# A rebuilt front of a hybrid mixer kernel: half of the first modulation on TensorE, low weight halves on VectorE, the residual's scale and bias rows on GpSimd in one block

## What is computed

```python
x = layer_norm(x, ln0_g, ln0_b)
mod = silu(c) @ ada_w + ada_b
sh1, sc1, g1, sh2, sc2, g2 = split(mod, 6)
h = x * (1.0 + sc1) + sh1
z = h @ w_in
y = concat([pool_mixer(z[:, :512]), rglru_mixer(z[:, 512:1024], z[:, 1024:])]) @ w_out
x = layer_norm(ALPHA * x + g1 * y, ln1_g, ln1_b)
h = x * (1.0 + sc2) + sh2
y = peer(h, wq, k1, k2, u, v)
x = layer_norm(ALPHA * x + g2 * y, ln2_g, ln2_b)
```

## Time and profile before

| | us |
|---|---|
| median of three runs | 1901.21 (1898.95 to 1901.32) |
| the profiled execution, device time | 1901.77 |
| its span in the trace | 1900.0 |
| TensorE busy in the span | 1766.3 |
| VectorE busy in the span | 1218.4 |
| ScalarE busy in the span | 633.8 |
| GpSimd busy in the span | 604.3 |

### The profile page before, as it was taken

One profiled execution on the slowest core, in us unless ns is written; L12 is line 12 of the kernel. 1 busy time (PEld: TensorE's weight loads), 2 busy tenths in 40 slices (PEclk: granted clock), 3 DMA queues, 4 the chain that ended last, 5 costly groups with the idle time before them and its releaser, 6 DMA issues.

```text
span 1900.0 us, 24874 instructions
## 1 busy us (share of the span) xinstructions
PE 1766.3 (93%) x8396; PEld 1433.9 (75%) x8396; DVE 1218.4 (64%) x2200; ACT 633.8 (33%) x809; POOL 604.3 (32%) x266
## 2 busy tenths in 40 slices
PE   2779889998989998999999999999999999999994
PEld 2565468887867777878888888888888888888883
DVE  7995879999979980035555555555555555555567
ACT  1215133323269982232222222222222222222221
POOL 1541245383410013452222333333322223333333
PEclk9889989999989999999999999999999999999997
DMA  9433330043339997453444343344444444333311
GB/s 384 188 142 156 114 122 1 28 148 129 126 107 285 280 283 267 150 199 150 150 149 148 142 138 137 141 139 149 149 149 149 149 149 146 135 132 147 144 38 45
DMA packets 136109, 288.89 MB, mean 152 GB/s; under 512 B 8160, under 2 KB 73824, under 8 KB 133376
## 3 DMA queue, kind: packets, MB, share of 16 engines
q1 hardware_dynamic: 134352, 283.15, 42.4%
q0 software_dynamic: 1424, 4.85, 0.7%
q10 hardware_dynamic: 288, 0.29, 0.0%
HBM read 235.83 MB, written 52.43 MB: 152 GB/s over the span
## 4 chain that ended last, share of the span: by engine, by line
PE 53%; DVE 2%; ACT 0%; issue 0%; DVEq 0%; ACTq 0%
PE bank L778 18%; PE bank L780 18%; PE bank L779 18%; DVE acc L1410 0%; DVE xt L1438 0%; DVE w_full L1351 0%; DVE st L1439 0%; DVE nmean L1427 0%; DVE w_full L1434 0%; DVE xt L1413 0%; ACT xt L745 0%; DVE xt L1447 0%; DVE acc L1367 0%; DVE xt L1448 0%; DVE u_lo L1308 0%
## 5 line engine op out<-in xcount | busy, mean ns | idle before, releaser
L489 POOL TENSOR_TENSOR v_lo<-v_raw,v_hi 128x1024 fp32r<-128x1024 f32 x128 | 307.7, 2426 | 719.9 <-ACT v_hi L691 719.9
L778 PE MATMUL bank<-h_hi,u_hi 128*128 128x512 f32 x1248 | 499.1, 400 | 15.7 <-POOL u_lo L484 11.3
L780 PE MATMUL bank<-h_hi,u_lo 128*128 128x512 f32 x1248 | 492.1, 394 | 0.0
L779 PE MATMUL bank<-h_lo,u_hi 128*128 128x512 f32 x1248 | 492.0, 394 | 0.0
L1367 DVE TENSOR_TENSOR acc<-acc,bank 128x512 f32<-128x512 f32 x496 | 329.2, 685 | 148.6 <-PE bank L780 148.5
L778 PE MATMUL bank<-v_hi,w_hi 128*128 128x512 f32 x1024 | 400.3, 391 | 8.9 <-DVE w_lo L1361 7.9
L779 PE MATMUL bank<-v_lo,w_hi 128*128 128x512 f32 x1024 | 399.8, 390 | 0.0
L780 PE MATMUL bank<-v_hi,w_lo 128*128 128x512 f32 x1024 | 399.8, 390 | 0.0
L691 ACT ACTIVATE v_hi<-v_raw 128x1024 fp32r<-128x1024 f32 x128 | 128.5, 1052 | 545.5 <-PE bank L780 545.5
L1351 DVE TENSOR_TENSOR w_full<-gelu_out,gate_in 128x512 f32<-128x512 f32 x64 | 45.2, 706 | 384.9 <-ACT gelu_out L707 214.4
L778 PEld LDWEIGHTS bank<-h_hi,u_hi 128*128 128x128 f32 x1248 | 238.5, 191 | 67.6 <-POOL u_lo L484 11.6
(11 more groups left out here) (171 smaller groups left out, 1691.9 us busy)
## 6 DMA issues: line engine op xcount, KB each, us to landing
u_raw<-ut_dram SPq DMA_DIRECT2D x128, 512.0 KB, 3.3
v_raw<-v_dram SPq DMA_DIRECT2D x128, 512.0 KB, 5.8
gate_in<-gates_dram SPq DMA_DIRECT2D x64, 512.0 KB, 6.9
wbuf<-ada_w_dram SPq DMA_DIRECT2D x12, 2048.0 KB, 14.5
early_dram<-gelu_out SPq DMA_DIRECT2D x64, 256.0 KB, 2.2
gates_dram<-wbuf SPq DMA_DIRECT2D x4, 4096.0 KB, 16.0
gates_dram<-arena SPq DMA_DIRECT2D x4, 4096.0 KB, 16.0
early_in<-early_dram SPq DMA_DIRECT2D x64, 256.0 KB, 6.2
```

What stands on the lines that cost most here:

```text
L489: pool.tensor_tensor(v_lo[:, s, :], v_raw[:, s, :], v_hi[:, s, :].bitcast(F32), ALU.subtract).then_inc(s_vlo, 1)
L778: pe.matmul(out, a_hi, b_hi, start=(k == 0), stop=False)
L779: pe.matmul(out, a_hi, b_lo, start=False, stop=False)
L780: return pe.matmul(out, a_lo, b_hi, start=False, stop=(k == n - 1))
```

## The change

The front is written anew on every engine; the queries, the ranking, the scatter and the main loop stand as they were.

- Ada pieces 0 to 3: VectorE weighs chunks 0 to 3 only. TensorE takes chunks 4 to 7 as products of one column straight from the piece (`upper_modulation`, 16 products a piece). The two sums are added.
- The low halves of the 12 z weight tiles are made by VectorE (`low_weights_of`), and a third buffer exists for tile 2. ScalarE makes the full h of every other chunk. z 0 and z 1 are computed together, chunk by chunk; four banks instead of two hold z.
- GpSimd has during z only the 8 `affine` instructions, as one block, from the end of the first transposes on.
- Gates of the recurrence, ada 4 and 5 and the rest are interleaved with z; ada 4 to 9 all go through slot 3. Gelu is applied where z 8 to 11 leave their banks. The product of gate i and the convolved x goes from GpSimd to VectorE.
- Ada 6 to 9 are spread over the mixer output. The second h is made in two parts: three token blocks, then the last.
- Ada 10 and 11, the second gate, go to the stage of 20 expert tiles, with their DMAs behind the second tile of that stage. The zeroing of `acc` goes there too, from GpSimd to VectorE.

```diff
-PIECES = ([("ada", j) for j in range(4)] + [("win", 1), ("ada", 4), ("ada", 5), ("win", 0), ("ada", 6), ("ada", 7)]
-          + [("win", 2), ("ada", 8), ("ada", 9), ("wout", 0), ("wout", 1), ("ada", 10)]
-          + [("wq", 0), ("ada", 11), ("wq", 1), ("wq", 2), ("wq", 3)])
+PIECES, SLOT_OF = zip(
+    (("ada", 0), 0), (("ada", 1), 1), (("ada", 2), 2), (("ada", 3), 3),
+    (("win", 1), 0), (("win", 0), 1), (("win", 2), 2), (("ada", 4), 3), (("ada", 5), 3),
+    (("wout", 0), 1), (("ada", 6), 3), (("wout", 1), 2), (("ada", 7), 3), (("wq", 0), 0),
+    (("ada", 8), 3), (("ada", 9), 3), (("wq", 1), 3), (("wq", 2), 1), (("wq", 3), 2))
+NSPLIT = 4
+HALF_K = KD // 2
+MOD_UPPER = 64
...
 SLOTS = 4
-SLOT_OF = [n % SLOTS for n in range(len(PIECES) - 5)] + [0, 3, 1, 2, 3]
 CAND_A = 4 * K
 CAND = CAND_A + (K - 4) * 4
...
             for n, (name, j) in enumerate(PIECES):
                 slot = SLOT_OF[n]
-                if (name, j) in (("win", 0), ("wq", 3)):
-                    sp.wait_ge(s_hlo, KD if name == "win" else 2 * KD)
-                if slot in SLOT_OF[:n]:
+                if (name, j) == ("wq", 0):
+                    sp.wait_ge(s_lru, 1)
+                elif slot in SLOT_OF[:n]:
                     sp.wait_ge(*used_up(max(m for m in range(n) if SLOT_OF[m] == slot)))
                 sp.dma_start(piece_buf[:, slot], src[name][j]).then_inc(s_piece[slot], 16)
...
+                if s == 1:
+                    sp.wait_ge(s_scmm, 4 + S // 4)
+                    for g in range(2):
+                        sp.dma_start(late_ada[g], ada_w[10 + g]).then_inc(s_late[g], 16)
...
             def affine(nth, n):
                 if n == 0:
-                    pool.wait_ge(s_tr, KD * (nth + 1))
+                    pool.wait_ge(s_tr, 3 * KD if nth else KD)
                     pool.wait_ge(s_rows, 32 * (nth + 1))
...
             def lo_weights(n):
                 pool.wait_ge(s_wthi, n + 1)
                 pool.tensor_tensor(u_lo[:, n % 2], weights(n), u_hi[:, n % 2].bitcast(F32), ALU.subtract
                                    ).then_inc(s_wtlo, 1)
-            lo_weights(0)
-            lo_weights(1)
+            pool.wait_ge(s_piece[0], 32)
+            load_rows("ln0_g", "ln0_b")
+            load_gate_bias("gate1_b")
             for n in range(2 * TB):
                 affine(0, n)
-                lo_weights(n + 2)
-            for n in range(2 * TB + 2, NZ):
-                lo_weights(n)
             pool.wait_ge(s_x0, TB)
             load_rows("ln1_g", "ln1_b")
...
             centre(0)
+            centre(1)
+            pool.wait_ge(s_wtlo, NZ)
+            lo_weights(NZ)
+            lo_weights(NZ + 1)
             pool.wait_ge(s_ymm, 2 * TB)
             pool.wait_ge(s_yres, 2 * TB)
             load_gate_bias("gate2_b")
...
+            def upper_modulation(j):
+                wait_piece(pe, "ada", j)
+                for m in range(4):
+                    for k in range(HALF_K, KD):
+                        pe.matmul(bank[7][:, 4 * j + m:4 * j + m + 1], piece("ada", j)[:, k, m * P:(m + 1) * P],
+                                  silu_c[:, k:k + 1], start=(k == HALF_K), stop=(k == KD - 1))
...
-            transposes(0, BANKS_X, range(4))
-            for j in range(4):
-                modulation(j)
-            transposes(0, BANKS_X, range(4, KD))
-            for n in range(12):
-                pe.wait_ge(s_wtlo, n + 1)
-                if n >= 2:
-                    pe.wait_ge(s_zev, n - 1)
-                for k in range(KD):
-                    if n == 0:
...
+            transposes(0, BANKS_X, range(len(BANKS_X)))
+            pe.wait_ge(s_silu, 1)
+            upper_modulation(0)
+            modulation(0)
+            upper_modulation(1)
+            modulation(1)
+            upper_modulation(2)
+            modulation(2)
+            upper_modulation(3)
+            modulation(3)
...
+            pe.wait_ge(s_wtlo, 2)
+            for k in range(KD):
+                if k + len(BANKS_X) < KD:
+                    transposes(0, BANKS_X, range(k + len(BANKS_X), k + len(BANKS_X) + 1))
+                pe.wait_ge(s_hlo, k + 1)
+                z_chunk(0, k)
+                z_chunk(1, k)
...
+            z_tiles(2, 6)
...
+            mixer_output(0, range(NG))
+            mixer_output(1, range(NG))
+            mixer_output(0, range(NG, KD))
+            mixer_output(1, range(NG, KD))
+            modulation(6)
+            modulation(7)
+            mixer_output(2, range(KD))
+            mixer_output(3, range(KD))
+            modulation(8)
+            mixer_output(4, range(KD))
+            mixer_output(5, range(KD))
+            modulation(9)
+            mixer_output(6, range(KD))
             transposes(1, BANKS_H)
-            pe.wait_ge(s_yres, 2 * TB)
-            modulation(10)
-            modulation(11)
+            mixer_output(7, range(KD))
+            pe.wait_ge(s_sc, 2)
+            transposes(2, BANKS_L)
...
                 expert_inputs(0, c, BANKS_SCATTER[c % GT], c - (GT - 1))
+                if c == T_RANK + T_SCATTER + AT_GATE2:
+                    pe.wait_ge(s_scev, 4 + S // 4)
+                    modulation(10)
+                    modulation(11)
...
+            def partial_modulation(j, chunks=range(KD)):
...
+                end = HALF_K if j < NSPLIT else KD
+                for k in chunks:
...
+            def low_weights_of(n):
+                hi, lo = split_of(n)
+                ve.wait_ge(s_wthi, n + 1)
+                ve.tensor_tensor(lo, weights(n), hi.bitcast(F32), ALU.subtract).then_inc(s_wtlo, 1)
...
             for j in range(4):
-                partial_modulation(j)
+                partial_modulation(j, range(HALF_K))
+            low_weights_of(0)
             read_mod(0, 16, 4)
+            link(ve.tensor_tensor(mod[:, 0:16], mod[:, 0:16], bank[7][:, MOD_UPPER:MOD_UPPER + 16], ALU.add))
             scales(0, 8, "ln0_g", "ln0_b", scale1, bias1)
-            low_input(0, BANKS_X, scale1, bias1)
-            partial_modulation(4)
-            partial_modulation(5)
+            low_input(0, BANKS_X, scale1, bias1, range(0, 1))
+            low_weights_of(1)
+            low_input(0, BANKS_X, scale1, bias1, range(1, KD))
+            low_weights_of(2)
             ve.wait_ge(s_expl, 1)
...
-            add_gate_row(0)
-            partial_modulation(6)
-            partial_modulation(7)
+            low_weights_of(3)
+            low_weights_of(4)
+            ve.wait_ge(s_wtlo, 4)
+            convolve((0, 1))
+            low_weights_of(5)
+            convolve((2, 3))
+            low_weights_of(6)
+            partial_modulation(4, range(HALF_K))
+            low_weights_of(7)
+            partial_modulation(4, range(HALF_K, KD))
+            partial_modulation(5)
...
+            add_gate_row(0)
             for g in range(NG):
                 ve.tensor_tensor(bufs[g + 1][:, g, PAD_P:2 * PAD_P], ramp[:, g, :], zp[:, g, PAD_P:2 * PAD_P],
                                  ALU.subtract).then_inc(s_pooly, 1)
...
+                ve.wait_ge(s_zev, NZ - 4 + c + 1)
+                ve.tensor_tensor(y_lru[:, c, :], gr[:, c, :], zg[:, c, :], ALU.mult).then_inc(s_lru, 1)
+            partial_modulation(6)
+            partial_modulation(7)
...
+            ve.wait_ge(s_rowg, 2)
+            residual(0)
+            partial_modulation(8)
+            residual(1)
+            partial_modulation(9)
+            link(head_means(0))
+            scaled_means(0)
+            residual(2)
+            read_mod(24, 40, 10)
+            scales(24, 32, "ln1_g", "ln1_b", scale2, bias2)
+            low_input(1, BANKS_H, scale2, bias2)
+            link(head_means(1))
+            scaled_means(1)
+            residual(3)
+            low_input(2, BANKS_L, scale2, bias2)
...
+            link = Chain(ve, s_cg).link
+            partial_modulation(10)
+            ve.wait_ge(s_part, GATE_PIECES[2] + 1)
+            ve.memset(acc[:, :, :], 0.0).then_inc(s_zacc, 1)
+            partial_modulation(11)
+            add_gate_row(1)
```

More of the change, by code:

```diff
@@ L845, in queries @@
                     for k in range(KD):
-                        if first:
-                            pe.wait_ge(s_hlo, KD + k + 1)
+                        if first and half == 0:
+                            pe.wait_ge(s_hlo, 2 * KD + k + 1)
                         mm = thrice(bank[half][:, :], k, KD, ((u_hi[:, half, k, :], u_lo[:, half, k, :]),
@@ L1114, in _, with convolve @@
-            add_gate_row(0)
-            partial_modulation(6)
-            partial_modulation(7)
+            def convolve(channels):
+                for t in range(CONV_W):
+                    for c in channels:
+                        w = vec("conv_w", 4 * t + c)
+                        shifted = zx[:, c, PAD_C - CONV_W + 1 + t:PAD_C - CONV_W + 1 + t + S]
+                        if t == 0:
+                            ve.wait_ge(s_zev, c + 1)
```

(30 more changed lines are left out.)

365 lines of the change are left out of this document (189 added, 176 removed).

## The result

The changed kernel takes 1904.99 us, median of 9 runs (1903.05 to 1906.53), beside 1900.69 for the kernel before on the same chip (9 runs, 1898.78 to 1902.12). The ratio is 1.0024, with a 95% interval of 1.0014 to 1.0033: slower by 4.6 us. The forecast was 1900 us, with chances of 0.44 for faster by over 0.2%, 0.34 for the same and 0.22 for slower. The profiled execution has a span of 1903.5 us, 3.5 more than before.

A forecast was written before the change was run, and what follows sets the result against it. The front was taken to wait for VectorE, with a microsecond won at the first query a microsecond of the whole. 1901.8 - 4.1 (front) + 1.7 (gate sums) + 1 (load) = 1900.4, taken as 1900; range 1884 to 1908.

The forecast's parts named there:

- Scale rows: Front's start: with TensorE's one-column records at the lower clock level, rows ready at 55 us, 9 later than before.
- The 36 and the 18: Scale rows: us that all 160 one-column records take at the lower and at the upper clock level.
- the 3 us of credit: Scale rows: 3 us taken off for one-column records directly behind the transposes, still at the upper clock level.
- The block on GpSimd: Front, during z: eight instructions of 2.4 us, taking turns with VectorE one for one, from 65 until about 87.
- TensorE's wait before z 3: Front: TensorE idles 11.6 us after z 2 ends at 78.7, then starts z 3 slowly.
- the wait for ada 7: Mixer output: ada 7 ready 7.6 us after issue at 168; a TensorE wait at L805 of 7 or more shows it.
- First query: Front's end: first query starts at 246.6 against 250.75 before, 4.1 us earlier.
- the distance to the first ranking: From first query to first ranking: should stay 28 us.
- The clock rival: Front: clock stays up through one-column products, scale rows 14 us earlier than walked, total 1887; chance 0.25.
- The stage of 20 tiles: Gate sums +1.7 us, 4 MB load +1 us; ada 10 and 11 and the zeroing hidden under VectorE's idle 87.8.
- The store rival: Stage of 20 tiles: the new load holds up gelu stores, ScalarE waits 10 to 14 us, total 1912; chance 0.13.
- GpSimd's block costs nothing: Front: VectorE gets its small instructions in between, z 3 would not wait, 11 us earlier there, total 1891; chance 0.09.

The follow-up runs named there:

- h3: The changed kernel unaltered, measured once more on the same chip as another run: 1906.38 us, ratio 1.0038 to the kernel before.
- g1: On top of e3: VectorE weighs ada 0 to 3 whole, TensorE does no one-column products of upper halves: 1887.00 us, ratio 0.9934.
- g3: On top of e3: the 17 small decay instructions of VectorE moved ahead of the scale rows: 1888.94 us, ratio 0.9945.
- h1: On top of e3: two unread products of 512 columns behind each of the 16 groups of one-column products: 1908.88 us.
- g2: On top of e3: one unread product of 256 columns behind each of the 16 groups of one-column products: 1908.95 us, ratio 1.0041.
- e3: Changed kernel with the 4 MB loaded in four 1 MB parts behind tiles 5, 7, 9, 11, gate sums behind tile 16: 1896.80 us, ratio 0.9983.
- e4: Changed kernel with e3's spread load and the zeroing of acc in 8 pieces, one behind each chunk of ada 11: 1900.02 us, ratio 0.9992.

## Why the prediction was wrong

Its time, 1900, was 5 us short, and with it the sign. By its own steps:

- *Scale rows*: 55 predicted, 55.95 seen. That it is so close has some luck in it: the 160 one-column records took 34.1 us at the lower level where 36 were reckoned, and the 3 us of credit did not come in this execution. The 36 and the 18 are about 160 times the record of the earlier trace rows and of the earlier trace rows, 0.23 and 0.115 us. That the level falls through one-column products was the author's assumption there; rows 4 alone do not show it. In its place stands h3: the first 32 records took 3.72 us, the next 32 of the same line 6.97. The block on GpSimd 65 to 87, seen 65.7 to 86.2; TensorE's wait before z 3 11.6, seen 10.0; the wait for ada 7 7.6, seen 7.8 on VectorE and 3.8 of it on TensorE at L805, where 7 or more was to show it, so this mark failed while the piece was 1.3 us early. First query 4.1 us earlier, seen 4.5; the distance to the first ranking fell from 28.3 to 27.3 us. The front was right in mechanism and nearly in size, and g1 and g3 each took away the cause that it named and got the time back.
- *The clock rival* (1887) did not occur: the one-column records of the first modulation took 0.21 to 0.23 us. h1 and g2 show that what TensorE did there decided the level (0.12 us a record against 0.21). Only the 3 us of credit behind the transposes come and go: in this trace the first 32 records take 6.83 us, in h3's 3.72, with the same code. TensorE's busy time does not tell the two levels apart: in h3 TensorE was busy for 8.00 of 8 us from 30 to 38, and the granted clock was 0.50; in h1 it was busy for 32.00 of 32 us, at 0.12 us a record.
- *The stage of 20 tiles* is the step that failed. The sum had +1.7 for the gate sums (seen 1.77) and +1 "between none and 14" for the 4 MB. The 4 MB and the zeroing together cost 8.2 in one stall. Two things were missing. The slack was counted in buffers (four tiles of `u`, two gelu buffers), not in time: the low half of `u` has 1.4 us to spare per tile, and the store was 3.7 us late. And the zeroing and ada 11 were put under VectorE's 87.8 idle us at no cost: they cost VectorE nothing, but with ada 11 ready behind the zeroing, a low half that TensorE waits for was held for 3.5 us. It is the same loss of turns that the front's walk had priced one for one; I had not asked the question in the stage where GpSimd is the engine with the deadline. A VectorE instruction on 4 columns took 2.36 us beside GpSimd in the front, as priced. The stage fits that only in part: the low half was held for 3.5 us, from far ahead of the 0.36 us in which ada 11's first instruction ran, while beside the zeroing alone it took its usual 2.40 (e3).
- *The store rival* (1912) had the mechanism for half of it, and was priced too high: a wait of 10 to 14 us, where the gelu was 3.7 late. Its chance of 0.13 was too low. The point that decides it was stated (10.9 us for what stands ahead in the queue) and had its answer in the rows: 4 MB had held an issue for 12.2 us.
- *GpSimd's block costs nothing* (1891): refuted by g3, which won 7.2 us by moving 17 instructions out of it.

Open is what the rest of e4's 3 us is, what exactly claims GpSimd's turn during the zeroing, and about 1 us that the changed kernel wins between the first ranking (5.5 ahead) and 718 (6.45 ahead), whose cause is not shown.

## What to carry to other kernels

A load that is put into a queue between stores with a rhythm has to be cut to what that rhythm leaves free: 4 MB at once cost 8 us together with the zeroing that fell behind them, 4 times 1 MB nothing. Idle time of VectorE is free for VectorE, but what is put there can also take GpSimd's turn (3.5 us here), so look at what GpSimd has to deliver then, and place small instructions where GpSimd rests. Before work is moved to TensorE in one-column products, price them at the length that a row of them has in the trace (0.21 us a record here, not 0.115): the 128 records that were to relieve VectorE put the start off by 12 us, and a split of 6 to 2 was better than 4 to 4.

## What the runs showed of the hardware

Through one-column products without a gap TensorE here lost the upper level that it had behind the transposes, and stayed at the lower (h3: 32 records in 3.72 us, then 0.21 each, 39 in 8 us at a granted clock of 0.50). With two products of 512 columns behind every 8 records they ran at 0.12 us (h1), with one of 256 at 0.21 (g2, 8 in 1.71). In the changed kernel the column of the granted clock shows 1.00 beside the same 39 records in 8 us. First h3, then the changed kernel:

```profile
30.00:38.00 8.00, 8.00 (x39) 8.00 (x39) 2.74 (x4) 0.00 (x0) 0.00 (x0) 0.50 0.94 358
...
46.00:54.00 8.00, 8.00 (x39) 8.00 (x39) 0.00 (x0) 0.00 (x0) 0.00 (x0) 1.00 1.01 414
```

That column reads 1.00 there up to 80 us, also from 60 to 63, where a product of 512 columns takes 0.63 us as at the lower level. In the changed kernel's trace the length of a record tells more than that column.

A zeroing of 128x4096 on VectorE (3.47 us) left a GpSimd instruction beside it at its 2.40 us when VectorE had nothing ready behind it (six traces), and stood beside one held for 2.5 to 3.5 us when the first instruction of ada 11 was ready behind it (four traces; 4.9 to 5.9 us in place of 2.4).
